# Contraction rows of small products in a two-layer mLSTM and latent-attention encoder: one kind padded to 128, three kinds gathered

## What is computed

```python
# mLSTM, in blocks of frames
b = jnp.cumsum(lf, axis=-1)
D = jnp.where(causal, b[..., :, None] - b[..., None, :] + ig[..., None, :], -jnp.inf)
m = jnp.maximum(b + m0[..., None], jnp.max(D, axis=-1))
S = jnp.einsum('bhtd,bhsd->bhts', q, k) * jnp.exp(D - m[..., None])
...
# latent attention
q = (rmsnorm(cq, g_q_norm) @ w_uq).reshape(B, S, A_HEADS, NOPE_DIM + ROPE_DIM)
kn, v = expand_kv(ckv, w_ukv)
s = (jnp.einsum('bqhd,bkhd->bhqk', qn, kn) + jnp.einsum('bqhd,bkd->bhqk', qr, kr)) * ATTN_SCALE
p = jax.nn.softmax(jnp.where(mask, s, -jnp.inf), axis=-1)
```

## Time and profile before

| | |
|---|---|
| median of 3 runs | 2938.61 us (2929.41 to 2940.33) |
| the profiled execution | 2939.65 us, span 2937.8 us |
| PE busy | 2871.6 us, 98% of the span |
| PEld busy | 2660.4 us, 91% |
| DVE, POOL, ACT busy | 1608.8, 1482.6, 985.9 us |
| mean granted TensorE clock | 0.989 |

### The profile page before, as it was taken

The page is one execution under the profiler, slowest core; times in us unless marked ns, Lnnn a source line. Parts: engine busy times, 40 slices in busy tenths (PEclk is TensorE's granted clock), DMA queues, the critical chain, the costliest instruction groups (busy, mean ns, idle before and its releaser), DMA issues.

```text
span 2937.8 us, 45844 instructions
## 1 busy us (share of the span) xinstructions
PE 2871.6 (98%) x17057; PEld 2660.4 (91%) x17057; DVE 1608.8 (55%) x2161; ACT 985.9 (34%) x1926; POOL 1482.6 (50%) x1186
## 2 busy tenths in 40 slices
PE   8999999999999999999899999999999999999998
PEld 7999967779999999999789998677889999999997
DVE  7433345644765555655783333456457655655566
ACT  4222234432233333333341223244332333333333
POOL 2223242234367888887422222332333788888782
PEclk9999989999999999999999999799999999999999
DMA  5121210021211111111322112100212111111113
GB/s 167 42 41 33 38 39 1 1 88 51 84 41 50 50 57 43 57 43 43 110 88 54 31 31 38 31 1 1 95 44 95 44 43 57 43 57 43 52 48 133
DMA packets 211566, 154.92 MB, mean 53 GB/s; under 512 B 40856, under 2 KB 195112, under 8 KB 210672
## 3 DMA queue, kind: packets, MB, share of 16 engines
q1 hardware_dynamic: 194304, 111.29, 14.3%
q10 hardware_dynamic: 17136, 41.89, 3.8%
HBM read 128.56 MB, written 24.59 MB: 52 GB/s over the span
## 4 chain that ended last, share of the span: by engine, by line
PE 32%; issue 24%; POOLq 23%; POOL 13%; DVE 5%; ACT 2%; DVEq 1%; ACTq 0%; DMA 0%
PE acc L776 7%; PE acc L780 7%; PE acc L779 7%; POOL slab_lo L692 5%; POOLq L709 3%; POOLq L704 3%; POOLq L699 3%; POOL slab_raw L710 2%; POOLq L713 2%; POOLq L719 2%; POOLq L716 2%; POOL small_lo L692 2%; POOLq L722 2%; POOLq L655 1%; DVE residual L2161 1%
## 5 line engine op out<-in xcount | busy, mean ns | idle before, releaser
L557 POOL TENSOR_TENSOR slab_hi<-slab_raw,ones 128x1024 fp32r<-128x1024 f32 x63 | 123.5, 1961 | 680.5 <-PE acc L776 514.0
L692 POOL TENSOR_TENSOR slab_lo<-slab_raw,slab_hi 128x512 fp32r<-128x512 f32 (+1 forms) x376 | 414.2, 1110 | 101.9 <-ACT slab_hi L1948 66.4
L776 PE MATMUL acc<-act_hi,slab_hi 128*128 128x352 f32 x1296 | 426.6, 329 | 8.2 <-ACT residual L1672 5.2
L780 PE MATMUL acc<-act_lo,slab_hi 128*128 128x352 f32 x1296 | 416.4, 321 | 0.0
L779 PE MATMUL acc<-act_hi,slab_lo 128*128 128x352 f32 x1296 | 415.7, 321 | 0.0
L1948 ACT ACTIVATE slab_hi<-slab_raw 128x512 fp32r<-128x512 f32 (+1 forms) x372 | 193.4, 544 | 394.6 <-DMA slab_raw<-in_w_ffn_in 153.0
L1330 PE MATMUL acc<-act_hi,slab_hi 128*128 128x352 f32 x992 | 322.1, 325 | 0.9 <-ACT small_lo_f L1980 0.5
L1333 PE MATMUL acc<-act_hi,slab_lo 128*128 128x352 f32 x992 | 318.2, 321 | 0.0
L1334 PE MATMUL acc<-act_lo,slab_hi 128*128 128x352 f32 x992 | 317.8, 320 | 0.0
L2737 DVE TENSOR_TENSOR branch<-acc,branch 128x704 f32<-128x704 f32 x288 | 256.7, 891 | 88.3 <-PE acc L1398 74.0
L692 POOL TENSOR_TENSOR small_lo<-slab_raw,small_hi 128x256 fp32r<-128x256 f32 (+1 forms) x224 | 217.7, 976 | 115.2 <-ACT small_hi L1948 79.8
(11 more groups left out here) (511 smaller groups left out, 7349.7 us busy)
## 6 DMA issues: line engine op xcount, KB each, us to landing
slab_raw<-in_w_ffn_in SPq DMA_DIRECT2D x152, 256.0 KB, 2.9
slab_raw<-in_w_in SPq DMA_DIRECT2D x40, 512.0 KB, 3.9
slab_raw<-in_w_ffn_out SPq DMA_DIRECT2D x80, 256.0 KB, 2.5
x_spill<-residual ACTq DMA_DIRECT2D x2, 4224.0 KB, 12.4
residual<-x_spill ACTq DMA_DIRECT2D x2, 4224.0 KB, 14.1
f_spill<-residual ACTq DMA_DIRECT2D x2, 4224.0 KB, 11.5
slab_raw<-in_w_out SPq DMA_DIRECT2D x16, 512.0 KB, 4.5
slab_raw<-in_w_ffn_in SPq DMA_DIRECT2D x12, 512.0 KB, 3.7
```

Source lines behind the costliest of these rows:

```text
L557: pool.tensor_tensor(hi, raw, ONES[:, 0:1].broadcast_to([P, SLAB]), ALU.mult)
L692: pool.tensor_tensor(lo, QUAD[q][:, c0:c1], hi, ALU.subtract).then_inc(unit_ready, 1)
L776: mm = pe.matmul(out, wh, HH[:, x], start=k == 0, stop=False)
L780: mm = pe.matmul(out, wh, HL[:, x], start=False, stop=k == KT - 1)
```

## The change

Four places change. `UHL` and `SPREAD` get 128 partitions, all cleared or zero but for the rows of before, and L916 contracts over 128 rows. `latent_rows` takes the chunks of a step together: first all their 128-row transposes, then all the 32-row ones. The 16 products of L1105 all stand behind value tile 3. The three products of L1123 of a half stand behind the L1122 of its third key group.

```diff
-        UHL, SPREAD = home("u_hi_lo", W0, TP, F32R, 40), home("spread", W0 + TP, 8, F32R, 40)
+        UHL, SPREAD = home("u_hi_lo", W0, TP, F32R), home("spread", W0 + TP, 8, F32R)
...
-                            pe.matmul(bank(3 + h, 3 * P), SPREAD[:, 2 * p + h:2 * p + h + 1].broadcast_to([40, P]), UHL[:, t], start=True, stop=False)
+                            pe.matmul(bank(3 + h, 3 * P), SPREAD[:, 2 * p + h:2 * p + h + 1].broadcast_to([P, P]), UHL[:, t], start=True, stop=False)
...
-                def latent_rows(c):
-
-                    w = P if c < CH - 1 else DEC
-                    b = 3 + c % 4
-                    if c >= 4:
-                        pe.wait_ge(nat_staged, l * CH + c - 3)
-                    for j in range(2):
-                        pe.transpose(bank(b, P, (0, w), j * P), X[:, (2 + j) * T + c * P:(2 + j) * T + c * P + w], IDN[:, :])
-                    pe.transpose(bank(b, ROPE, (0, w), 2 * P), KRF[:, c * P:c * P + w], IDN[64:96, 64:96]).then_inc(nat_turned, 1)
+                def latent_rows(*cs):
+
+                    for c in cs:
+                        w = P if c < CH - 1 else DEC
+                        b = 3 + c % 4
+                        if c >= 4:
+                            pe.wait_ge(nat_staged, l * CH + c - 3)
+                        for j in range(2):
+                            pe.transpose(bank(b, P, (0, w), j * P), X[:, (2 + j) * T + c * P:(2 + j) * T + c * P + w], IDN[:, :])
+                    for c in cs:
+                        w = P if c < CH - 1 else DEC
+                        pe.transpose(bank(3 + c % 4, ROPE, (0, w), 2 * P), KRF[:, c * P:c * P + w], IDN[64:96, 64:96]).then_inc(nat_turned, 1)
...
-                        for c in ((1, 2), (3, 4, 5), (6, 7, 8))[i - 1]:
-                            latent_rows(c)
+                        latent_rows(*((1, 2), (3, 4, 5), (6, 7, 8))[i - 1])
...
-                    for h in (2 * kt, 2 * kt + 1) if kt < 4 else ():
-                        for k in range(2):
-                            mm = pe.matmul(bank(7, DEC, off=k * 256 + h * DEC), WUKT[:, (2 * h + k) * P:(2 * h + k + 1) * P],
-                                           QS[0:64, h * DEC:(h + 1) * DEC], start=True, stop=True)
                     if kt == 3:
+                        for h in range(HEADS):
+                            for k in range(2):
+                                mm = pe.matmul(bank(7, DEC, off=k * 256 + h * DEC), WUKT[:, (2 * h + k) * P:(2 * h + k + 1) * P],
+                                               QS[0:64, h * DEC:(h + 1) * DEC], start=True, stop=True)
                         mm.then_inc(sq_proj, 1)
...
-                        mm = pe.matmul(out, QS[64:96, e * P:(e + 1) * P], KRF[:, SEQ + n * TG:SEQ + (n + 1) * TG], start=False, stop=True)
                         if n == NG - 1:
+                            for i in range(NG):
+                                mm = pe.matmul(bank(3 * (1 - e) + i, TG), QS[64:96, e * P:(e + 1) * P], KRF[:, SEQ + i * TG:SEQ + (i + 1) * TG],
+                                               start=False, stop=True)
                             mm.then_inc(ss_scores, 1)
...
-                dve.tensor_tensor(SPREAD[:, :], IDN[0:40, 0:8], IDN[0:40, 32:40], ALU.add)
+                dve.tensor_tensor(SPREAD[:, :], IDN[:, 0:8], IDN[:, 32:40], ALU.add)
```

## The result

The changed kernel takes 2913.77 us (median of 12 runs, 2905.86 to 2917.6), the kernel before 2931.84 us in its own 12 (2921.3 to 2942.07). The ratio is 0.9936, 95% interval 0.992 to 0.9952: 0.64% faster, 18 us. The forecast was 23.7 us, counted down to 2915 us from a median of three runs of before that lay 7 us above the median of twelve. That the time came within 2 us of 2915 is therefore luck; the saving itself was over-estimated by 5.6 us.

The account below looks back on a forecast made before the run. TensorE, busy 98% of the span, was taken as the bound. Parts of 14.3 + 1.2 + 2.3 + 1.9 = 19.7 us plus 4 us of clock gave 23.7 us less: 2915 us from the median, range 2904 to 2925.

Parts of the forecast that it names:

- Part 1: Mixer decay-row products (L916): padding 40 to 128 rows removes row-size changes of 0.20 us each; 14.3 us less.
- Part 2: Set-up, latent_rows: gathered transposes save row-size changes, the last group gaining nothing because of ACT's staging; 1.2 us less.
- Part 3: Set-up, absorbed query (L1105): three of four pairs of row-size changes go in each layer; 2.3 us less.
- Part 4: Sample scores (L1123): 1.6 us a layer saved, about 0.6 returned waiting on DVE's reduction; 1.9 us less in all.
- The clock: Set-up: half-clock stretches end sooner under a dense run of value products; 4 us less, bounds 0 and 8.
- 24 such products (10 us at half clock) run without a break from about 405.4: Set-up: unbroken 512-column products bring full clock back 3.4 to 6.8 us after the run begins.
- case B: Whole kernel: row-size changes vanish but half-clock stretches stay as long; 19.7 us less, chance 0.27.
- A: Whole kernel: row-size changes vanish and the clock returns earlier; 24 us less, chance 0.55.
- C: Mixer: ACT's emptying of the banks holds groups 1 and 2 in every pair; 11.6 us less, 2927, chance 0.11.
- D: Cost belongs to L916 and L1123 themselves, not the size change; only L1105 and L1072 gain, 3 us, chance 0.04.
- E: Mixer: activity falls and each of 24 groups brings a clock drop; 17 us slower, 2956, chance 0.03.
- Rule weighed: TensorE: skill says loads overlap running matmuls only when row group differs, so saving 0; the trace was taken to disagree.

Follow-up runs that it names:

- e8: Changed kernel plus four filler products in both set-up stalls and, in each layer's last head pair, ACT copying before squaring: 2904.07 us, ratio 0.991.
- e2: Kernel before with only the set-up edits (latent rows, L1105, L1123 gathered), mixer as before: 2922.28 us, ratio 0.9969.
- e7: Kernel before with only the 64-row products of L1105 gathered behind value tile 3: 2926.05 us, ratio 0.9983.
- e11: The changed kernel run again unaltered, beside the kernel before on another chip: 2911.92 us, ratio 0.9918.
- e5: Kernel before with only the latent_rows edit, transposes gathered by row size: one run, 2920.19 us.
- e3: Kernel before, still 40 rows unpadded, each mixer call's two 40-row products placed side by side before its 128-row ones: 2921.75 us, ratio 0.9968.
- e12: Kernel before with only four filler products in the stall ahead of chunk 0's latent transposes in each layer: 2922.56 us, ratio 0.997.

## Why the prediction was right, and which term was off

- **Part 1, 14.3 us: right.** In the profiles the pairs shortened by 2.07, 2.08, 2.02 and 0.78 in layer 0 and about the same in layer 1, 7.0 a layer for the predicted 7.1; alone it was 14.2 us at a like clock. The bank that ACT holds took what the prediction gave it: 0.61 from copy to resumption, and all of the gain in the last pair. e8 shows that this was ACT's squaring, and nothing else.
- **Part 2, 1.2 us: 1.5** (2 x 0.74), read at full clock, where it was worked out at half. The wait on ACT's staging came (1.07).
- **Part 3, 2.3 us: 1.9**, for the same reason: I had priced part of it at half clock.
- **Part 4, 1.9 us: 1.6.** The wait on DVE's reduction came: 0.45 of idle TensorE in front of the first maximum, 0.67 counted in starts, where the prediction had 0.6. The gross gain is then 0.81 + 0.67 = 1.5 a layer for its 1.6.
- **Sum without the clock, 19.7 us: 18.7** at a mean clock of 0.991 (lines through 63 runs of before and 18 of the changed kernel: 2931.8 and 2913.1).
- **The clock, 4 us: the least certain term, and its mechanism was not what happened.** The mean clock is 0.9910 over 63 runs of before (standard error 0.0003) and 0.9918 over 18 of the changed kernel (0.0006): 1.4 to 1.8 us at 1.7 to 2.2 us for 0.001, and not told apart from 0. The kernels that share its set-up or its block do better: on the three chips of the experiments e2, e7 and e11 lie 0.0022, 0.0021 and 0.0017 above before beside them, and all 42 runs of the four have 0.9925 (0.0004), worth about 3 us. So the gathering seems to raise the clock by something between none and all of the 4 us; the changed kernel's own first 12 runs, at 0.9912, hardly show it.
- **The step that failed in it** was "24 such products (10 us at half clock) run without a break from about 405.4", from which an earlier rise followed. In none of the 8 layers of the four kernels with the block and without fillers was the clock still at half at the first value product, so the dense run never had a rise to hasten. I forecast stretches of 17 and 23 us and found 0 and 13.65, all of it ahead of the value tiles. And I overlooked what stands behind the run: the 16 gathered products of 32 columns, 3.7 us for no more columns than two value products have, which take 0.46, and in or behind which the clock falls again in 8 of 12 layers. What ended the stretches sooner stays open. One pointer: without fillers, a stretch reached the value tiles in 7 of the 10 layers whose latent rows were not gathered, and in none of the 8 whose rows were; but e5, which has this edit alone, had one run.
- **The sum.** 23.7 us were forecast, 18 measured by the medians of 12 runs each, 20 by the means of 63 and 18 runs. Of these 4 to 6 us the four sums hold 1, the clock term the rest. So case B (no clock gain) was nearer to the measured time than A.
- **Rivals.** C fell with the pairs' 2.07 us: ACT holds groups 1 and 2 only by 0.1. D fell with e3. E did not occur: no profile of the study shows half clock in the mixer's pairs.
- **Rule weighed.** Loads of 128-row products start under running 128-row products, in the changed kernel for L916 too (119.50). The Trainium skill's rule in "TensorE: Matmul & The Clock Gate", Part 3, The mechanism, that loads overlap only when the row group differs, would have had nothing saved; the measured 14 us decide against it. The Trainium skill, "TensorEngine Tiling (Array Packing)", Key Properties, says that a change of the tiling mode drains TensorE. The saving agrees with that, and e3 with 0.21 us a change; that what stands behind the price is a drain, no run here shows.

## What to carry to other kernels

Count, in program order, where products of up to 64 contraction rows stand beside 128-row ones; here each border cost 0.20 us of TensorE, and padding with zero rows or putting equals side by side removed it at no price in columns. Then look at what the time was covering: here a bank that ACT empties took 4 us of the mixer's 19 back, and swapping two ACT instructions returned 3.8. Before gathering many short products into one block, read the granted clock behind it, and compare kernels at a like mean clock, since one profile of each was 13 us off in this case.

## What the runs showed of the hardware that was not expected

- An idle stall of about 1 us was worth filling here. Four products of the identity with itself in each layer's stall of 0.93 us made the kernel before 9 us faster: mean clock 0.9954 against 0.9911 (e12).
- A run's time follows its mean granted clock closely: 2.2 us for each 0.001 over 63 runs of before, from 0.987 to 0.997, with 94% of their variance. In the 18 runs of the changed kernel it is 1.7, so the gain at a like clock depends on the clock: 18.7 us at 0.991, about 16.6 at 0.995.
- In or within 1 us behind a block of 16 products of 32 columns, in 32 instructions over 3.7 us, the clock fell to 1.2 GHz for 3.4 us or more in 8 of 12 layers; with the same products in four blocks of 1.0 us, or two of 1.8, it fell in none of the 9 layers that came there at full clock.
